# Delta-rule inverse on 32x32 diagonal blocks instead of 64x64 chunks, and part of the gate's SiLU placed beside the gate projection

## The reference, cut to what matters

```
    A = jnp.where(strict, jnp.einsum('bhncd,bhned->bhnce', k_beta, k) * decay, 0.0)
    eye = jnp.eye(C, dtype=jnp.float32)
    u = lax.linalg.triangular_solve(eye + A, v * beta[..., None], left_side=True,
                                    lower=True, unit_diagonal=True)
    w = lax.linalg.triangular_solve(eye + A, k_beta * jnp.exp(gc)[..., None], left_side=True,
                                    lower=True, unit_diagonal=True)
...
    o = rmsnorm(o, out_norm) * jax.nn.silu(gate.reshape(B, S, H, dv).astype(jnp.float32))
```

## Time and profile before

| | |
|---|---|
| median of 3 runs | 3202.23 us (3200.82 to 3203.06) |
| span of the profiled execution | 3203.1 us, 0.9 us above the median of the runs |
| PE busy | 3156.9 us, 99% of the span |
| DVE, ACT, POOL busy | 2094.1, 1666.8 and 194.3 us |
| DMA | 537.09 MB, 168 GB/s on average |
| first stretch of L2185 (turn 0) | from 1332.76 us to 1364.18 us of the span |
| second stretch (turn 1) | from 2929.1 us to 2960.6 us |

### The profile page before, as it was taken

One profiled execution on the slowest core, in us unless ns is written; L12 is line 12 of the kernel. 1 busy time (PEld: TensorE's weight loads), 2 busy tenths in 40 slices (PEclk: granted clock), 3 DMA queues, 4 the chain that ended last, 5 costly groups with the idle time before them and its releaser, 6 DMA issues.

```text
span 3203.1 us, 52367 instructions
## 1 busy us (share of the span) xinstructions
PE 3156.9 (99%) x20480; PEld 2760.0 (86%) x20480; DVE 2094.1 (65%) x2310; ACT 1666.8 (52%) x2006; POOL 194.3 (6%) x183
## 2 busy tenths in 40 slices
PE   9999999999999999999999999999999999999999
PEld 7888888888888889988888988888878888899888
DVE  6677766666666667566666666666766666675665
ACT  5456544545545546454454454554555454464543
POOL 0000001000001300400000000000610000004000
PEclk9999999999999999999999999999999999999999
DMA  6744555554355555235555555555514556551354
GB/s 228 233 142 152 190 192 168 185 189 146 127 195 166 200 185 159 69 107 196 189 188 187 184 181 187 178 199 186 182 49 143 186 174 203 174 163 65 125 190 144
DMA packets 416142, 537.09 MB, mean 168 GB/s; under 512 B 23052, under 2 KB 361180, under 8 KB 415760
## 3 DMA queue, kind: packets, MB, share of 16 engines
q1 hardware_dynamic: 414220, 528.76, 49.8%
q0 software_dynamic: 1792, 6.49, 0.9%
HBM read 534.13 MB, written 1.05 MB: 167 GB/s over the span
## 4 chain that ended last, share of the span: by engine, by line
PE 91%; DVE 4%; ACT 4%; issue 1%; DMA 0%; SPq 0%; ACTq 0%; DVEq 0%
PE banks L444 29%; PE banks L449 15%; PE banks L179 9%; PE banks L180 9%; PE banks L181 9%; PE banks L853 8%; PE banks L1481 3%; PE banks L2185 2%; ACT w_hi L119 1%; DVE w_lo L127 1%; PE banks L1559 1%; PE banks L1241 1%; PE banks L1571 1%; PE banks L346 1%; DVE xT L301 0%
## 5 line engine op out<-in xcount | busy, mean ns | idle before, releaser
L127 DVE TENSOR_TENSOR w_lo<-raw,w_hi 128x2048 fp32r<-128x2048 f32 x506 | 1164.0, 2305 | 263.0 <-ACT w_hi L119 262.8
L119 ACT ACTIVATE w_hi<-raw 128x2048 fp32r<-128x2048 f32 x505 | 962.1, 1909 | 151.9 <-PE banks L181 58.4
L444 PE MATMUL banks<-xT,w_hi 128*128 128x512 f32 x4224 | 1007.0, 391 | 1.3 <-DVE xT L301 1.0
L444 PEld LDWEIGHTS banks<-xT,w_hi 128*128 128x128 f32 x4224 | 782.4, 188 | 160.4 <-issue 2.7
L449 PEld LDWEIGHTS banks<-xT,w_lo 128*128 128x128 f32 x4224 | 540.7, 191 | 19.6
L449 PE MATMUL banks<-xT,w_lo 128*128 128x256 f32 x4224 | 549.0, 283 | 0.0
L537 ACT ACTIVATE xn<-banks 128x512 f32<-128x512 f32 x264 | 157.4, 596 | 625.2 <-PE banks L449 624.1
L179 PE MATMUL banks<-w_hi,hid_hi 128*128 128x512 f32 x960 | 375.2, 391 | 0.0
L180 PE MATMUL banks<-w_lo,hid_hi 128*128 128x512 f32 x960 | 375.2, 391 | 0.0
L181 PE MATMUL banks<-w_hi,hid_lo 128*128 128x512 f32 x960 | 373.7, 389 | 0.0
L545 ACT ACTIVATE hid_hi<-hid 128x512 fp32r<-128x512 f32 x120 | 75.8, 632 | 345.0 <-PE banks L181 336.9
(11 more groups left out here) (461 smaller groups left out, 2866.8 us busy)
## 6 DMA issues: line engine op xcount, KB each, us to landing
raw<-ffn_w_gate_up SPq DMA_DIRECT2D x352, 512.0 KB
raw<-ffn_w_down SPq DMA_DIRECT2D x264, 512.0 KB
raw<-ffn_w_up SPq DMA_DIRECT2D x88, 512.0 KB
raw<-ffn_w_gate SPq DMA_DIRECT2D x86, 512.0 KB
raw<-gdn_w_in SPq DMA_DIRECT2D x64, 512.0 KB
raw<-sc_w_in SPq DMA_DIRECT2D x24, 512.0 KB
raw<-nsa_w_in SPq DMA_DIRECT2D x20, 512.0 KB
raw<-rg_w_in SPq DMA_DIRECT2D x20, 504.0 KB
```

Source lines behind the costliest of these rows:

```text
L119: c.nc.scalar.activation(c.w_hi[r][:], c.raw[r][:], ACT.Copy).then_inc(c.sem("w_hi_split"), 1)
L127: c.nc.vector.tensor_tensor(c.w_lo[r][:], c.raw[r][:], c.w_hi[r][:].bitcast(F32), ALU.subtract).then_inc(c.sem("w_lo_split"), 1)
L444: tensor.matmul(out.rearrange("p (h n) -> p h n", h=2), c.w_hi[r][:, at], c.xT[:, :, k, :], start=k == 0, stop=False)
```

## The change

The levels stop at 16, on compact 32x32 diagonal blocks. `bY`, `bX`, `bT`, `bA` and `Am` hold 32 columns for each matrix instead of 64. A batch now has 32 products of 32x32 by 32x32 (`block_products`), four blocks of partitions in turn, each on its own diagonal 32x32 part of the array; consecutive ones alternate between two PSUM banks by `g % 2 ^ flip`. The last level (32) is done only for the lower left 32x32 corner of each 64x64 inverse (`corner_products`): one batch of 16 small products for `A X`, one that moves the `Y` of the second block through PSUM by a product with the identity, one for the corner itself, for each group. POOL clears the 64-wide `Y`, ACT copies the first block's rows into it, and DVE copies the other columns from PSUM. `bX` is now updated before `bY`, each with its own count of the semaphore. DVE gathers the diagonal blocks of A with four more copies of 32 partitions per group.

ACT applies SiLU to the first three gate slabs right after the small exponential beside slab 2, and to the last slab where the whole gate was done before.

```diff
-LEVELS = (1, 2, 4, 8, 16, 32)
+G_BLOCK = G_CHUNK // 2
+LEVELS = (1, 2, 4, 8, 16)
...
+def block_quads():
+
+    for flip in range(2):
+        for h4 in range(4):
+            for g in range(P // G_BLOCK):
+                yield g % 2 ^ flip, g, h4
...
-    def small_products(b, lo, pair, lhs, rhs):
-        for t, ch, h4 in quads():
-            z, r = 8 * b + 4 * t + h4, rows_of(ch)
-            last = mm(c.bank[2 * pair + t][r, lo + h4 * G_CHUNK:lo + (h4 + 1) * G_CHUNK], lhs(r, z), rhs(r, z),
+    def block_products(b, lo, pair, lhs, rhs):
+        for t, g, h4 in block_quads():
+            z, r = 8 * b + 4 * t + h4, block_rows(g)
+            last = mm(c.bank[2 * pair + t][r, lo + h4 * G_BLOCK:lo + (h4 + 1) * G_BLOCK], lhs(r, z), rhs(r, z),
                       start=True, stop=True)
         return last
+    def corner_products(b, pair, to, lhs, rhs):
+        for t, ch, h4 in quads():
+            z, r, out = 8 * b + 4 * t + h4, block_rows(2 * ch + 1 - to[0]), block_rows(2 * ch + to[1])
+            last = mm(c.bank[2 * pair + t][out, h4 * G_BLOCK:(h4 + 1) * G_BLOCK], lhs(r, z), rhs(r, z),
+                      start=True, stop=True)
+        return last
...
+    for b in range(2):
+        pe.wait_ge(c.sem("gdn_X"), 16 * u + 12 + 2 * b + 1)
+        corner_products(b, 2 + b, (1, 1), lambda r, z: v.AQ[r, z, 1, G_BLOCK:], lambda r, z: v.bX[r, z, :]
+                        ).then_inc(c.sem("gdn_ax"), 1)
+        pe.wait_ge(c.sem("gdn_X"), 16 * u + 12 + 2 * b + 2)
+        corner_products(b, b, (0, 1), lambda r, z: c.ident[r, r], lambda r, z: v.bY[r, z, :])
+    for b in range(2):
+        pe.wait_ge(c.sem("gdn_T"), 14 * u + 10 + b + 1)
+        corner_products(b, b, (0, 0), lambda r, z: v.bT[r, z, :], lambda r, z: v.bY[r, z, :]
+                        ).then_inc(c.sem("gdn_y"), 1)
...
+            act.wait_ge(c.sem("projection_read"), gate.step + 3)
+            early = v.gate[:, :, 0:3 * PCOLS]
+            scalar.activation(early, early, ACT.Silu)
...
         if m == 1:
-            scalar.activation(v.gate[:], v.gate[:], ACT.Silu).then_inc(c.sem("gdn_silu_gate"), 1)
+            late = v.gate[:, :, 3 * PCOLS:4 * PCOLS]
+            scalar.activation(late, late, ACT.Silu).then_inc(c.sem("gdn_silu_gate"), 1)
...
+        for n in range(P // G_BLOCK):
+            r = block_rows(n)
+            last = copy(A[r], group(v.AQ, b)[r, :, 1, G_BLOCK * (n % 2):G_BLOCK * (n % 2 + 1)])
+        chain(last)
```

More of the change, by code:

```diff
@@ L1930, in gdn_views @@
         vb = arena(c, 10240, P, G_MATS, G_DIM)
-        T = arena(c, 12288, P, G_MATS, G_CHUNK)
-        Am = [arena(c, 13312 + 1024 * j, P, G_MATS, G_CHUNK) for j in range(2)]
+        bT = arena(c, 12288, P, G_MATS, G_BLOCK)
+        bA = arena(c, 12800, P, G_MATS, G_BLOCK)
+        Am = [arena(c, 13312 + 1024 * j, P, G_MATS, G_BLOCK) for j in range(2)]
         E = arena(c, 15360, P, G_MATS, G_CHUNK)
@@ L1943, in gdn_views @@
         upper, lower = masks[:, 0:128], masks[:, 128:256]
-        level = [masks[:, 256 + 64 * m:320 + 64 * m] for m in range(6)]
-        inclusive, ident = masks[:, 640:704], masks[:, 704:768]
+        level = [masks[:, 256 + G_BLOCK * m:256 + G_BLOCK * (m + 1)] for m in range(len(LEVELS))]
+        ident = masks[:, 608:640]
+        inclusive = masks[:, 640:704]
         taps = small(P, 24, G_TAPS)
@@ L2044, in pool_gdn @@
     level(4)
-    level(5)
+    for b in range(2):
+        g.memset(group(v.Y, b), 0.0).then_inc(c.sem("gdn_A_level"), 1)
     pool.wait_ge(c.sem("gdn_silu_gate"), u + 1)
@@ L2073, in blocks @@
                              pattern=[[b, P // b], [0, b]], channel_multiplier=-1))
-    for m, b in enumerate(LEVELS):
+    for m, b in enumerate((*LEVELS, G_BLOCK, G_CHUNK)):
         blocks(v.full[m], b)
-    blocks(v.full[6], G_CHUNK)
     step(g.affine_select(out=v.upper, in_=v.full[6], compare_op=ALU.is_ge, fill=0.0, base=0,
@@ L2081, in pool_gdn_masks @@
                          pattern=[[-1, P]], channel_multiplier=1))
-    for m in range(len(LEVELS) - 1):
+    for m in range(len(LEVELS)):
         step(g.tensor_tensor(out=v.full[m], in0=v.full[m + 1], in1=v.full[m], op=ALU.subtract))
-    step(g.tensor_tensor(out=v.full[5], in0=v.full[6], in1=v.full[5], op=ALU.subtract))
     for m in range(len(LEVELS)):
@@ L2087, in pool_gdn_masks @@
     step(g.tensor_scalar(v.full[0], v.full[0], -1.0, None, ALU.mult))
[L2088 to L2092, removed]
+    for dst, src in [(v.level[m], v.full[m]) for m in range(len(LEVELS))] + [(v.ident, c.ident[:])]:
+        for q in range(P // G_BLOCK):
+            step(g.tensor_copy(dst[block_rows(q), :], src[block_rows(q), block_rows(q)]))
+    for ch in range(2):
+        rows = slice(G_CHUNK * ch, G_CHUNK * (ch + 1))
+        step(g.tensor_copy(v.inclusive[rows, :], v.upper[rows, rows]))
     assert made[0] == GDN_MASK_STEPS
@@ L2372, in act_gdn @@
             act.wait_ge(c.sem("gdn_ax"), 12 * u + 2 * m + b + 1)
-            scalar.activation(group(v.T, b).rearrange("p (t h) s -> p t (h s)", t=TOKS), pair_half(c, b, 0), ACT.Copy
-                              ).then_inc(c.sem("gdn_T"), 1)
+            copy_blocks(v.bT, b)
         if m == 1:
-            scalar.activation(v.gate[:], v.gate[:], ACT.Silu).then_inc(c.sem("gdn_silu_gate"), 1)
+            late = v.gate[:, :, 3 * PCOLS:4 * PCOLS]
+            scalar.activation(late, late, ACT.Silu).then_inc(c.sem("gdn_silu_gate"), 1)
+    for b in range(2):
+        act.wait_ge(c.sem("gdn_ax"), 12 * u + 10 + b + 1)
+        copy_blocks(v.bT, b, scale=-1.0)
+    for b in range(2):
+        act.wait_ge(c.sem("gdn_A_level"), 10 * u + 8 + b + 1)
+        act.wait_ge(c.sem("gdn_X"), 16 * u + 12 + 2 * b + 2)
+        for ch in range(2):
+            r = block_rows(2 * ch)
+            last = scalar.activation(group(v.Y, b)[r, :, 0:G_BLOCK], group(v.bY, b)[r], ACT.Copy)
+        last.then_inc(c.sem("gdn_T"), 1)
     act_load_sqrt(c)
@@ L2517, in dve_gdn @@
         for b in range(2):
-            Y, X = (group(a, b).rearrange("p (t h) s -> p t (h s)", t=TOKS) for a in (v.Y, v.X))
+            Y, X = (group(a, b).rearrange("p (t h) s -> p t (h s)", t=TOKS) for a in (v.bY, v.bX))
             dve.wait_ge(c.sem("gdn_y"), 10 * u + 2 * (m - 1) + b + 1)
[L2520 to L2526, removed]
+            dve.wait_ge(c.sem("gdn_x"), 8 * u + 2 * (m - 1) + b + 1)
+            tt(X, X, pair_blocks(c, 2 + b, 256), ALU.subtract).then_inc(c.sem("gdn_X"), 1)
+            tt(Y, Y, pair_blocks(c, b, 0), ALU.subtract).then_inc(c.sem("gdn_X"), 1)
+    for b in range(2):
+        dve.wait_ge(c.sem("gdn_y"), 10 * u + 8 + b + 1)
+        dve.wait_ge(c.sem("gdn_A_level"), 10 * u + 8 + b + 1)
+        corner = by_tile(group(v.Y, b))[:, :, :, G_BLOCK:]
+        copy(corner, pair_blocks(c, b, 0).rearrange("p t (h s) -> p t h s", s=G_BLOCK)
+             ).then_inc(c.sem("gdn_inverse"), 1)
     for s in range(1, gate.steps):
```

52 lines of the change are left out of this document (29 added, 23 removed).

## The result

| | before | after |
|---|---|---|
| median | 3202.64 us (3200.82 to 3203.96, 4 runs) | 3251.14 us (3249.16 to 3253.75, 4 runs) |
| ratio to before, 95% interval | | 1.0151 [1.0139, 1.0163] |
| stage of the inverse, turn 0 | 31.42 us | 54.02 us |
| the 64 records behind it, turn 0 | 3.71 us | 5.32 us |

What follows compares the result with a forecast made beforehand. PE was taken to bound the kernel, 90% of the stage being pitch; 20.6 + 1.2 = 21.8 us replaced 31.4 a turn, saving 19.2 in both: 3183.9 profiled, 3183.0 us as median, range 3173 to 3249.

Steps and rivals of the forecast that it cites:

- The forecast pitch: Time per 32x32 record on PE in the inverse: 11.1 ns taken, with 8.4 and 29.3 ns kept for the range.
- three in flight: In the inverse, records run on three array parts at once, giving 11.1 ns each; three or four in flight had chance 0.42.
- 1856 x 11.1 = 20.6 us: Products term for one turn of the inverse: 1856 records at 11.1 ns, in place of 960 records before.
- The stream itself is the limit: Rival: pairs reach PE no faster than 29.3 ns, so the inverse takes 54.4 us a turn, 3248 us in all; chance 0.35.
- the pace there is the same right behind a wait, when the queue is full, as later: Argument against the supply rival, from windows over the old stage: the pace looks like the array's limit, not the supply's.
- DMA is idle in these windows, so no transfer is in play.: Claim about the old inverse stage in both turns: DMA share is 0.02, so transfers do not matter there.
- The Trainium skill's floor: Page's claim that PE's start-to-start never falls below about 25 ns: 46.4 us a turn, 3232 us in all.
- Two in flight: Rival: bank sharing or ordered starts leave two records in flight at 16.7 ns, no change, 3202 us; chance 0.23 (15 to 19 ns).
- The clock: Sign of a wrong prediction: a granted clock below 1.00 in the new inverse stage, if PE's waits grow.
- Waits inside: PE's waits for copies and updates in the inverse: up to 1.2 us a turn; each level's 0.52 us wait goes.
- The excess of 0.88 over 0.52 us: PE's extra wait at the level behind the SiLU; moving the SiLU was to gain 0.4 us, already in the waits.
- its cover: ACT ahead of the weight split: 2.7 us of early SiLU and table load fit in 3.76 us idle, so cost nothing.

Runs made afterwards that it cites:

- e2: The changed kernel with the inverse's 32x32 products on the operands' upper halves as bfloat16, one record per call instead of two; 3198.09 us.
- e3: The changed kernel with only the first 16 of the 32 calls of each block batch; 3200.83 us.
- e8: The kernel before with early SiLU, `X` before `Y`, and two one-column bfloat16 products ahead of each 64x64 inverse call, 1920 pairs a turn; 3253.58 us.
- e9: The changed kernel with 64 more wide products a turn inside the stage, whose results nothing reads; 3253.87 us.
- e1: The changed kernel with the same products reordered, so that two of the four 32x32 parts take turns, then the other two; 3247.12 us.
- e4: The kernel before, 64x64 blocks kept, with early SiLU, `X` updated before `Y` with its own count, and `A X` in banks 4 to 7; 3199.34 us.
- e6: The kernel before with only the SiLU moved: three slabs early, the last where the whole was; 3202.3 us.
- e5: As e4, with the last level done only on the 32x32 corner, in place, 64 calls of 32x32 for 64 of 64x64; 3196.67 us.
- e7: As e4, with the inverse's products on the operands' upper halves as bfloat16, one record per call, 480 pairs a turn; 3175.59 us.

## Why the prediction was wrong, step by step

- **The forecast pitch, and "three in flight".** The step that failed is the multiplication 1856 x 11.1 = 20.6 us. It took the number of records in flight for what sets the pitch, and set the supply of instructions at nothing. The array did better than that, 8.5 ns in a burst of the profile after, but for 128 records at a time; over the stage it was 54.02 / 1856 = 29.1 ns. The runs e2, e3 and e8 show that the number of instructions sets it, and e9 that the array had time to spare.
- **The rival "The stream itself is the limit".** This is what happened, and its 3248 us was 3 short of the measured time. Its pitch was right by luck of numbers: 29.3 ns is the array's time for a 64-column record, 29.5 and 30.6 ns (turns 1 and 0) that of a piece by 128. Its sum missed by little because two errors partly cancel: the two stages grew by 44.5 us instead of 46, and L2249, which it left alone, by 4.0 us; without these 4.0 us the time would lie within the range. The kernel before used 128 pairs in 3.75 us, about as fast as pieces came in these runs (3.7 to 4.0 us on average; in e2 and e3 the fresh pieces began 3.95 and 4.0 us apart), and with what it had in hand and its 3.3 us of waits it showed no hole. I gave this rival 0.35 because "the pace there is the same right behind a wait, when the queue is full, as later". That excludes a supply much slower than 29.3 ns, not one about as fast, which shows only when the stock has run out.
- **"DMA is idle in these windows, so no transfer is in play."** Wrong, and it could have been read. The earlier trace rows has 4 GB/s there with no data moving; 960 pairs by 128 bytes in 31.42 us are 3.9 GB/s. That was the instruction queue, and its packets in the window, 7 of 16 KB, are shown above.
- **The Trainium skill's floor.** By "TensorE: Matmul & The Clock Gate" starts are never nearer than about 25 ns. The bursts have 8.5 ns, so no run here shows that floor; 3232 us was nearer to the result than 3183, but for another reason. The rule that bears on it is another one of the Trainium skill: "Runtime: NRT & Kernel Launch", "Instruction fetch mechanics", says that instructions are refilled in blocks of 16 KB, 256 instructions, and that the cost of crossing a block is mostly hidden. The block agrees with the 14 packets; the cost was hidden only where 128 pairs took PE about as long as a piece takes to come, 3.7 to 4.0 us, or longer.
- **Two in flight.** Refuted at its price of 16.7 ns: in the bursts, in which blocks 0 and 2 write one bank, a record took 8.5 ns, and even e1, with two parts at a time, had 10.8. Whether records that share a bank still hinder each other a little, no run tells.
- **The clock.** Named as a sign of being wrong, but not priced. It was 0.56 over the stage. In the stage it costs little, since a burst of 1.9 us still ends before the next piece; behind it, L2249 lost 1.6 and 2.4 us.
- **Waits inside.** `X` first takes away the 0.52 us, as said (e4: 0.28 us at one level turn, then none). The excess of 0.88 over 0.52 us does not come from the SiLU (e6). What makes it stays open; turn 1 of the kernel before has 0.52 at that place with the same SiLU. A hint: a q14 packet begins at 1341.6 us in turn 0, 0.7 us behind the late subtraction of DVE (1340.95 us), and there is none in that stage of turn 1; whose instructions q14 brings, no row tells.
- **ACT and DVE.** The rows after:

```profile
1328.73 1.49 ACT L2399 ACTIVATE mix_out<-mix_out 128x1536 f32<-128x1536 f32 x1
1331.18 1.91 ACT L119 ACTIVATE w_hi<-raw 128x2048 fp32r<-128x2048 f32 x1 [0.95 <-PE banks L181]
...
1334.21 0.38 ACT L2405 ACTIVATE arena<-banks 128x256 f32<-128x256 f32 x1 [0.57 <-PE banks L2202]
```

```profile
1328.01 1.18 DVE L2553 COPY arena<-arena 32x256 f32<-32x256 f32 x4
...
1331.12 0.69 DVE L2561 COPY mix_out<-banks 128x512 f32<-128x512 f32 x1 [0.68 <-PE banks L181]
1338.26 0.42 DVE L2576 TENSOR_TENSOR arena<-arena,banks 128x256 f32<-128x256 f32 x1 [6.45 <-PE banks L2202]
```

  The early SiLU left 0.95 us of idle time ahead of the split, so its cover held. A copy of 256 columns took 0.38 us (0.39 said), an update 0.42 (0.425 said), and the four copies 1.18 us together, where 1.7 was allowed: the slab's read was not late.

## What to carry to other kernels

Count the instructions of a stage against its time, not only its work: here PE got 128 weight load and matmul pairs in 3.7 to 4.0 us, 29 to 31 ns a pair, and once the 210 to 260 pairs in hand were used up no stage went faster, however small its products were. Smaller products paid where their number did not grow (e5's last level), and fewer products paid more (e7). A stream near the limit may show no hole; look at the instruction queue's packets in the window, and at what the transfer rate would be if every pair were fetched.

## What the runs showed of the hardware

- Beginnings of bursts came 3.9 and 3.8 us apart in the two turns after, whose bursts lasted 1.3 to 2.1 us, and 3.7 us apart in e1 with bursts of 2.4 us, while a packet's own transfer took 1.05 us. In the rows shown each packet began 0.7 to 1.9 us behind the beginning of a burst, in e1 while the burst still ran. That fits one piece at a time, asked for when the one before is begun.
- A packet of 16 KB was 128 pairs in every pair of runs: 1792 pairs and 14 packets more from before to after, 1920 and 15 more from before to e8, 1664 and 13 fewer from after to e3.
- In turn 0 after, 256 records passed before the first hole named `issue`, in turn 1 it was 212: about two pieces were in hand, although the stage ahead of it runs at 120 ns a pair and left time to fetch more.
- Four 32x32 parts ran at 8.5 ns a record at full clock, two at 10.8 (e1, one burst), so four parts instead of two bought only a fifth.
- A granted clock of 0.50 outlasted the last hole by 5.2 us of unbroken work in turn 0 and by 7.9 us in turn 1 (3002.69 to 3010.57 us), so a stage with holes charges the one behind it.
